# First feed-forward matrix in seven block products, its pairs taking turns with the second matrix's tiles, weight blocks added on VectorE

## The reference

```python
    x = x + mem_attend(rmsnorm(x, P['norm_mem']), mem_k, mem_v, P['mem_w_q'], P['mem_w_o'])
    h = rmsnorm(x, P['norm_ffn'])
    x = x + jnp.square(jax.nn.relu(h @ P['ffn_w1'])) @ P['ffn_w2']
```

## Time and profile before

| | |
|---|---|
| time, median of 3 runs | 1926.37 us (1924.69 to 1928.71) |
| span of the profiled execution | 1995.0 us, mean granted clock 0.878 |
| PE busy | 1911.0 us (96%) |
| DVE busy | 1020.3 us (51%) |
| ACT busy | 725.8 us (36%) |
| POOL busy | 105.2 us (5%) |
| first layer's feed-forward stage | about 608 to 1020 us |
| second layer's feed-forward stage | about 1591 to 1979 us |

### The profile page before, as it was taken

How to read it: one execution, slowest core, us unless ns; L and a number is a source line. 1 busy time by engine, 2 the same in 40 slices (tenths; PEclk the granted TensorE clock), 3 DMA queues, 4 the chain that set the end, 5 groups by cost and what they waited for, 6 DMA issues and landing times.

```text
span 1995.0 us, 37755 instructions
## 1 busy us (share of the span) xinstructions
PE 1911.0 (96%) x16626; PEld 1758.6 (88%) x16626; DVE 1020.3 (51%) x1741; ACT 725.8 (36%) x1268; POOL 105.2 (5%) x108
## 2 busy tenths in 40 slices
PE   6999998999999999999999999889999999999997
PEld 5985776999789999999999857769997999999996
DVE  6677665454335544344355776655543455353533
ACT  4434546452334221222234345453623432121222
POOL 2020000200010000000010200001000100000001
PEclk8888887888888888888888889989999999999998
DMA  5100000553112222222221000014520222222221
GB/s 218 59 17 1 4 24 24 194 171 104 33 64 75 85 85 85 85 75 87 83 78 60 19 1 3 3 46 155 194 85 22 85 85 88 93 85 85 96 85 56
DMA packets 38594, 149.52 MB, mean 75 GB/s; under 512 B 4384, under 2 KB 4544, under 8 KB 36768
## 3 DMA queue, kind: packets, MB, share of 16 engines
q1 hardware_dynamic: 36288, 131.05, 19.6%
q0 software_dynamic: 2144, 16.06, 2.2%
HBM read 139.68 MB, written 7.41 MB: 74 GB/s over the span
## 4 chain that ended last, share of the span: by engine, by line
PE 89%; DVE 4%; ACT 4%; issue 1%; POOL 1%; DMA 0%; DVEq 0%; SPq 0%; ACTq 0%; POOLq 0%
PE PS L651 82%; PE PS L789 5%; PE PS L1037 1%; ACT hH L1180 1%; POOL sq L577 1%; DVE stat L1968 1%; PE PS L1136 0%; DVE hL L1621 0%; DVE rs L1935 0%; DVE hT L1934 0%; ACT aP L1180 0%; ACT L1180 0%; POOL msq L629 0%; DVE wL L1607 0%; DMA mem<-mem_in 0%
## 5 line engine op out<-in xcount | busy, mean ns | idle before, releaser
L651 PE MATMUL PS<-hH,wH 128*128 128x272 f32 x2272 | 508.6, 307 | 32.2 <-DVE hL L1616 23.0
L651 PE MATMUL PS<-hH,wL 128*128 128x272 f32 x2272 | 488.7, 298 | 0.0
L651 PE MATMUL PS<-hL,wH 128*128 128x272 f32 x2272 | 488.3, 298 | 0.0
L651 PEld LDWEIGHTS PS<-hH,wH 128*128 128x128 f32 x2272 | 372.1, 194 | 51.9 <-issue 20.5
L1607 DVE TENSOR_TENSOR wL<-ring,wH 128x1024 fp32r<-128x1024 f32 x238 | 301.1, 1266 | 218.8 <-ACT wH L1180 218.4
L1180 ACT ACTIVATE wH<-ring 128x1024 fp32r<-128x1024 f32 x238 | 249.8, 1050 | 354.4 <-PE PS L651 352.7
L651 PEld LDWEIGHTS PS<-hH,wL 128*128 128x128 f32 x2272 | 370.3, 193 | 0.0
L651 PEld LDWEIGHTS PS<-hL,wH 128*128 128x128 f32 x2272 | 369.3, 193 | 0.0
L651 PE MATMUL PS<-hidH,wH 128*128 128x272 f32 x1024 | 216.6, 294 | 0.0
L651 PE MATMUL PS<-hidL,wH 128*128 128x272 f32 x1024 | 216.4, 293 | 0.0
L651 PE MATMUL PS<-hidH,wL 128*128 128x272 f32 x1024 | 216.2, 294 | 0.0
(11 more groups left out here) (322 smaller groups left out, 2630.6 us busy)
## 6 DMA issues: line engine op xcount, KB each, us to landing
ring<-wall SPq DMA_DIRECT2D x238, 512.0 KB, 3.3
lw<-lw_in POOLq DMA_DIRECT2D x2, 2240.0 KB, 9.6
xT<-x_in SPq DMA_DIRECT2D x4, 544.0 KB, 6.1
y_out<-hT SPq DMA_DIRECT2D x8, 272.0 KB, 2.1
mem<-mem_in POOLq DMA_DIRECT2D x2, 1024.0 KB, 5.1
mks<-mks_in POOLq DMA_DIRECT2D x2, 1024.0 KB, 10.5
mvs<-mvs_in POOLq DMA_DIRECT2D x2, 1024.0 KB, 13.4
memk_out<-mkp POOLq DMA_DIRECT2D x2, 1024.0 KB, 5.4
```

What stands on the lines that cost most here:

```text
L651: return e.matmul(out, lhsT=a, rhs=b, start=start, stop=stop)
```

## The change

The first feed-forward matrix is taken in pairs of output tiles, q = 0 to 15. A pair is a 2 x 2 block matrix (two halves of the 1024 inputs, two output tiles), and so are the activations (two halves of the inputs, two halves of the frames). Instead of eight block products the pair takes seven, on sums and differences of the blocks. A product is one unit: 4 blocks of 128 x 128, three products each, 272 frames, so 12 matmuls. The units are named M1, M5, M6, M2, M7, M4, M3 in the order in which they run; some go into the same PSUM bank on top of an earlier one, after ACT has copied out the sum so far.

- Weights: the pair's two loads (a, b) are split by halves of a tile. DVE computes four sums or differences of 128 x 512 numbers per pair (`combine`, called comb0 to comb3 below): one before each of M5, M6, M7, M3. Seven halves are split instead of two whole tiles. `wH` and `wL` now hold six halves.
- Ring: load a of a pair is given up after M2's half is split and after comb3; load b after M4's half. The next pair's load b takes the slot of this pair's load a.
- Activations: for each `mo` tile ACT writes two blocks (`up_raw`), DVE makes two differences (tiles 0 to 3) or three (tiles 4 to 7), ACT rounds and DVE subtracts the blocks (`up_hi`, `up_lo`). This takes the place of the eight `hH`, `hL` tiles behind `mo` 7.
- Results: ACT copies out of PSUM after M1, M6 and M7 (`f_a1`, `f_u2`, `f_u3`); DVE adds after M2, M7 and M3, and multiplies the positive part by `rs` in three instructions. ACT then squares twice (`squared`), once rounded and once not. DVE's `hid_lo` stays.
- Order: pairs 0 to 3 run alone, as M5 M6 M2 M7, M1 of the next pair, M4 M3. From pair 4 on two `f2` tiles stand in each pair: M1 M5 M6 M2 M7, f2, M4 M3, f2. The last eight `f2` tiles are as before.
- `lw` of the second layer is loaded after the first layer's last `f2` tile, in two parts, since its room now holds `hid`.

```diff
+def _ffn_units():
+    def up(q, *products):
+        return [("f1", 7 * q + j) for j in products]
+    units = up(0, M1)
+    for q in range(4):
+        units += up(q, M5, M6, M2, M7) + up(q + 1, M1) + up(q, M4, M3)
+    for q in range(4, PAIRS):
+        i = 2 * (q - 4)
+        units += (up(q, M1) if q > 4 else []) + up(q, M5, M6, M2, M7) + [("f2", i)] + up(q, M4, M3) + [("f2", i + 1)]
+    return units + [("f2", i) for i in range(8 * GROUPS - 8, 8 * GROUPS)]
...
+        def wait_raw_read(e, m):
+            l, (st, i) = m // NT, LOADS[m % NT]
+            if st != "f1":
+                e.wait_ge(w_lo, tile_no(l, st, i) + 1)
+            elif i % 2:
+                e.wait_ge(w_lo, tile_no(l, st, 7 * (i // 2) + M4) + 1)
+            else:
+                e.wait_ge(w_lo, tile_no(l, st, 7 * (i // 2) + M2) + 1)
+                e.wait_ge(s["comb"], at(l, "comb", 4 * (i // 2) + 4))
...
@@ tensor: up(l, i)
+                elif j == M6:
+                    e.wait_ge(s["f_a1"], at(l, "f_a1", q + 1))
+                elif j == M7:
+                    e.wait_ge(s["f_u2"], at(l, "f_u2", q + 1))
+                elif j == M4:
+                    e.wait_ge(s["f_u3"], at(l, "f_u3", q + 1))
+                else:
+                    e.wait_ge(s["f_c22"], at(l, "f_c22", q + 1))
...
@@ scalar
                 for i in range(8):
                     ahead(l, "mo", i)
-                    if i == 7:
-                        wait_tile(e, l, "mo", 7)
-                        for k in range(7):
-                            scaled_hi(l, "g_ffn", k)
                     wait_evac(e, l, "mo", i)
+                    up_raw(i)
                     square(3 * l + 2, i)
...
+                for st, i in FFN:
+                    ahead(l, st, i)
+                    if st == "f1":
+                        q, j = i // 7, i % 7
+                        if 0 < q < 5 and j in (M5, M6):
+                            squared(2 * (q - 1) + (j == M6))
+                        if (q, j) == (0, M7):
+                            rstd(3 * l + 2)
+                        if j in (M1, M6, M7):
+                            wait_tile(e, l, "f1", i)
+                            act(hid_part(q, j == M7, j != M1), up_bank(l, q, 0), ACT.Copy)\
+                                .then_inc(s[{M1: "f_a1", M6: "f_u2", M7: "f_u3"}[j]], 1)
...
@@ vector: combine(l, q, i)
+                if i == 0:
+                    wait_load(e, second)
+                    tt(sums[:, 0, :], raw_half(second, 0), raw_half(second, 1), ALU.add)\
...
+                elif i == 1:
+                    tt(sums[:, 1, :], sums[:, 0, :], raw_half(first, 0), ALU.subtract)\
...
+                elif i == 2:
+                    tt(raw_half(second, 0), raw_half(first, 0), raw_half(second, 0), ALU.subtract)\
...
+                else:
+                    tt(sums[:, 1, :], raw_half(first, 1), sums[:, 1, :], ALU.subtract)\
```

More of the change, by code:

```diff
@@ L68 @@
 N_IN = len(IN)
[L69 to L77, removed]
[L78 to L82 removed]
+DENSE = [(st, i) for st, n in (("in", N_IN), ("out", 8), ("mk", 8), ("mv", 8), ("mq", 8), ("mo", 8)) for i in range(n)]
@@ new lines, with _loads, _placed @@
+FFN = _ffn_units()
+UNIT_LIST = DENSE + FFN
+NU = len(UNIT_LIST)
+UNIT = {u: i for i, u in enumerate(UNIT_LIST)}
+def _loads():
+    loads = []
+    for st, i in UNIT_LIST:
+        if st != "f1":
+            loads.append((st, i))
+        elif i % 7 == M1:
+            loads += [("f1", 2 * (i // 7)), ("f1", 2 * (i // 7) + 1)]
+    return loads
+LOADS = _loads()
+NT = len(LOADS)
+LOAD = {t: i for i, t in enumerate(LOADS)}
+RING = 3
+HALVES = 6
+def _placed():
+    half, freed, parity, owner, at_, normal = [], [], [], [-1] * HALVES, 0, 0
+    for n in range(DEPTH * NU):
+        wide = UNIT_LIST[n % NU][0] != "f1"
+        at_ += wide and at_ % 2
+        mine = [at_ % HALVES] + [at_ % HALVES + 1] * wide
+        half.append(mine[0])
+        freed.append(max(owner[h] for h in mine))
+        for h in mine:
+            owner[h] = n
+        at_ += len(mine)
+        parity.append(normal % 2 if wide else None)
+        normal += wide
+    return half, freed, parity
@@ new lines @@
+HALF, FREED, PARITY = _placed()
+BEFORE = [max((m for m in range(n) if PARITY[m] == PARITY[n]), default=None) for n in range(DEPTH * NU)]
+FIRST_UNITS = [0, 1] + [l * NU + UNIT[("out", i)] for l in range(DEPTH) for i in range(2)]
+SPLITS_AT = {}
+for _u in range(DEPTH * NU):
+    if _u not in FIRST_UNITS:
+        SPLITS_AT.setdefault(FREED[_u] + 1, []).append(_u)
+EVAC_ENGINE = {st: "act" if st in ("mk", "mv") else "dve" for st, _ in UNIT_LIST}
+EVACUATED = [t for t in UNIT_LIST if t[0] != "f1" and (t[0] != "mv" or t[1] % 2)]
@@ L83, with evac_value @@
 EVAC_PER_LAYER = {e: sum(EVAC_ENGINE[t[0]] == e for t in EVACUATED) for e in ("act", "dve")}
-RUNS = [(0, N_IN), (N_IN, NT + N_IN), (NT + N_IN, 2 * NT)]
-def evac_value(layer, tile):
-    eng = EVAC_ENGINE[STREAM[tile][0]]
+def evac_value(layer, unit):
+    eng = EVAC_ENGINE[UNIT_LIST[unit][0]]
     return eng, layer * EVAC_PER_LAYER[eng] + sum(
-        EVAC_ENGINE[t[0]] == eng and t in EVACUATED for t in STREAM[:tile + 1])
+        EVAC_ENGINE[t[0]] == eng and t in EVACUATED for t in UNIT_LIST[:unit + 1])
@@ L569, in put, with add_squares @@
                 e.dma_start(out, src).then_inc(stored[kind], 16)
-            def add_squares(r):
-                for k in range(1, 8):
+            def add_squares(r, first=1, last=7):
+                for k in range(first, last + 1):
                     e.wait_ge(s["sq_ready"], 8 * r + k + 1)
@@ L727, in mem_product, with dense_steps @@
                     last.then_inc(pe_done, 1)
[L729 to L734, removed]
+            def dense_steps(l, st, one=None, h_from=0, first=0):
+                for i in range(first, {"in": N_IN}.get(st, 8)) if one is None else (one,):
+                    n = tile_no(l, st, i)
                     e.wait_ge(w_lo, n + 1)
-                    if n >= 2:
-                        eng, v = evac_value((n - 2) // NT, (n - 2) % NT)
+                    if BEFORE[n] is not None:
+                        eng, v = evac_value(BEFORE[n] // NU, BEFORE[n] % NU)
                         e.wait_ge(evac[eng], v)
@@ L1567, in _ @@
                     wait_evac(e, l, "mo", i)
+                    up_raw(i)
                     square(3 * l + 2, i)
[L1569 to L1587, removed]
+                    if i < 4:
+                        e.wait_ge(s["f_cross"], at(l, "f_cross", i + 1))
+                        up_hi(i, Q11, T2)
+                    else:
+                        e.wait_ge(s["f_turn"], at(l, "f_turn", 2 * i - 7))
+                        up_hi(i, T2, Q21)
+                        e.wait_ge(s["f_turn"], at(l, "f_turn", 2 * i - 6))
+                        up_hi(i, Q21, T4 + 1)
```

323 lines of the change are left out of this document (243 added, 80 removed).

## The result

| | before | after |
|---|---|---|
| time, median | 1927.54 us (1924.69 to 1930.62) | 1940.53 us (1937.07 to 1943.48) |
| ratio after / before | | 1.0067, 95% interval 1.0047 to 1.0088 |
| profiled execution: span, mean granted clock | 1995.0 us, 0.878 | 1935.3 us, 0.978 |

The change makes the kernel 13 us slower. I had forecast 1926 us, practically no change. The time lies in my range (1898 to 1944), but the slowdown, clear of the noise, is not what I had forecast. The profiled spans can't be compared, since the clocks differ.

A forecast was written before the change was run, and what follows sets the result against it. PE was taken as the bound. Fewer matmuls saved 25.5 us (first layer) and 24.0 (second), added stalls cost 17.4 and 23.7; twice the second layer's -0.3 gave 1926.4 - 0.6, 1926 us, range 1898 to 1944.

The forecast's parts named there:

- stage against before: First mo residual to last f2 residual of a layer; forecast net -8.1 us first layer, -0.3 second.
- the price of the mo tiles: DVE and ACT steps per mo tile: 5.2 us for tiles 0 to 3, 7.0 for 4 to 7, nothing for POOL's additions.
- The half clock: Rival, chance 0.12: after stalls PE's matmuls come 0.227 us apart, costing 5 to 8 us a layer; 1938 us.
- The slot of load b: In pairs 0 to 3 comb0 waits 3.3 us for load b; slower rival, chance 0.18: 4.2 or 5.3, 1934 to 1942 us.
- the list on DVE: DVE's instructions and waits in pairs 0 to 3 set the pace: 14.1 us a pair against PE's 10.5.
- the two long stalls: PE in the first pair waits for ACT's copies: 7.2 us ahead of M6, 6.4 us ahead of M4.
- the table loads: Two on ACT within rs, ahead of M7's copy, 1.28 us each, part of 3.95 us.
- the dense f2 phase: From pair 4 on, with two f2 tiles in each pair of 22.5 us: no PE loss.
- the late `lw`: Second layer's lw loads behind the first layer's last f2 tile; first used 12 us later, so costed at nothing.
- The drain of 1.38 us: The skill's drain at ACT table switches would lengthen M4's stall 2.8 us a layer, 1932 in all; forecast left it out.

The follow-up runs named there:

- e1: Changed kernel, but POOL's additions of squares in the mo tiles cover only 8 of 544 columns: 1930.43 us, ratio to before 1.0017.
- e5: The kernel before, unchanged, profiled once more: 1928.9 us, span 1926.8, clock 0.987.
- e2: Changed kernel, but in mo tiles 4 to 7 ACT squares behind its last rounding, so POOL adds later: 1942.85 us, ratio to before 1.0068.
- e9: Changed kernel, plus 44 matmuls of 128 columns on PE behind M1 of pair 1, ahead of M4: 1939.15 us, ratio to before 1.0055.
- e3: Changed kernel, but comb3 moved right behind comb2, so that load a's slot is free sooner: 1906.49 us, ratio to before 0.9877.
- three small moves: Changed kernel with comb3 right behind comb2, squares summed on PE, and rs made ahead of M6's copy: 1894.26 us, ratio to before 0.9824.

## Why the prediction was wrong

Times in the second layer, counted from M1's start (1523.14 in the changed kernel, t = 0 of the forecast):

| step | forecast | measured |
|---|---|---|
| 192 matmuls fewer, no loss from pair 4 on | 24.0 us saved | no gap; 0.1260 us a matmul for 0.1255 |
| mo tiles 0 to 3 | 5.2 us each | 5.2 |
| mo tiles 4 to 7 | 7.0 us each | 8.0 |
| M6 resumes | 9.9 | 13.6 |
| M4 resumes | 23.2 | 27.3 |
| DVE enters pair 1's list | 28.8 | 34.2 |
| pairs 1 and 2 | 14.1 us each | 14.7, 14.6; first layer 14.2, 14.1 |
| first f2 tile | 76.2 | 82.9; first layer 81.6 |
| stage against before | -0.3 us | +6.7 us; first layer +5.4 |

**The step that failed** is the price of the mo tiles. Of the 6.7 us by which the first f2 tile is late (5.4 in the first layer), 3.7 are there in both layers when M6 resumes. I had the row that tells it: DVE's instruction stretched from 1.23 to 1.55 us beside POOL. In its place I wrote "in the new order mostly one that waits for ACT anyway stands beside them, so I add nothing", and kept 1 us a layer for the range. It was 1.15 us in each of four tiles, 4.3 to 4.9 us a layer by e1. The 0.32 us of the row was no price per addition. It was what was left of the addition when DVE's instruction came. The pair of rows in the kernel before, profiled again (e5):

```profile
1488.79 1.36 POOL L577 TENSOR_TENSOR sq<-sq 128x544 f32<-128x544 f32 x1 [110.78 <-ACT sq L1180]
...
1489.69 1.54 DVE L1607 TENSOR_TENSOR wL<-ring,wH 128x1024 fp32r<-128x1024 f32 x1 [1.68 <-ACT wH L1180]
```

Here 0.46 us of the addition are left when DVE's instruction starts, and it loses 0.31. In the changed kernel 1.29 are left, and the third difference loses 1.16. In e2 it is 1.31 and 1.16. The new order has an instruction come 0.12 us behind the addition's start, so nearly all of it is left. With the stall ahead of M6 as it is, these microseconds go straight to the first f2 tile.

**The half clock** I had as a rival with a price of 5 to 8 us a layer. Behind M6's stall it lasts for 24 matmuls in both layers and costs nothing, since ACT's copy for M4 comes later still. Behind M4's stall it cost up to 1.7 us in the second layer and 0.1 in the first (e9). Behind the short stalls of pairs 1 to 3 it came once a layer, not in every pair. In the second layer that was in pair 1, for 16 matmuls, and the list on DVE hid all but 0.2 us. In the first it was in pair 3, for 14, and there DVE waits for PE at M3's sum, which it doesn't in the second layer's pair 3:

```profile
651.81 0.44 DVE L2363 TENSOR_TENSOR hT<-PS,hT 128x272 f32<-128x272 f32 x1 [0.68 <-PE PS L940]
...
1599.43 0.44 DVE L2363 TENSOR_TENSOR hT<-PS,hT 128x272 f32<-128x272 f32 x1
```

From DVE's entry into pair 3's list to the first f2 tile it is 20.4 us in the first layer and 19.4 in the second. I take the lower clock as the cause of this 1.0 us; no run takes it away by itself.

**The slot of load b** held in mechanism: comb0 stands for 1.9 to 2.3 us in each of the eight places. From comb3's end to comb0 it is 3.4 us in the first layer and 3.7 in the second, where I had 3.3; that makes the pairs 14.1 to 14.7 us long, and the rival's 4.2 and 5.3 didn't come. But e3 shows what I hadn't seen: the wait was there to be taken away by moving one instruction.

**Right** were the list on DVE and its 14 us a pair, what stands ahead of the two long stalls, the table loads, the dense f2 phase and the late `lw`. The loads take 1.28 us each, and the exponential starts 0.02 us behind the second. The drain of 1.38 us that the Trainium skill has there ("ScalarE: Activation LUTs", What ACT_TABLE_LOAD costs) isn't in this trace, as the forecast had said.

**The sum.** In the second layer the first f2 tile is 6.7 us late: 3.7 at M6, 0.4 more at M4 (the load's 3.6 us for 3.3), 1.3 more when DVE enters pair 1's list (the lower clock), and 1.3 in pairs 1 to 3, nearly all of it the load. In the first layer the same steps are 3.7, 0.3, 0.1 and 1.4, of which I put 1.0 down to the lower clock in pair 3. That makes 5.4, but for rounding.

**Not explained** is a small one: PE takes 6.055 us for an f2 tile in the changed kernel and 6.01 before, at the same granted clock of 1.00. The kernel before has 6.05 too in its mo tiles; only its f1 and f2 tiles take 6.01. Over the 2436 matmuls from the first to the last f2 residual that is 1.1 us a layer. With the 6.7 it is 7.8, against 7.0 missed in the second layer, and 6.5 against 5.7 in the first; the 0.8 between is open in both. I didn't try to find the cause.

## What to carry to other kernels

Where GpSimd works beside a dense list on VectorE whose operands lie in SBUF, price its instruction at its full length on that list, and look at who starts first in the new order, not at the stretch which the old order showed. A step that waits for a ring slot should free it as soon as its last reader can run: moving one subtraction up, to right behind comb2, was worth more than twice what the whole change had lost. And when a change turns a PE-bound stage into a chain over two engines, count the chain once more after each fix: here three small moves turned 13 us lost into 35 gained.

## What the runs showed of the hardware

- DVE and GpSimd took turns, whole instruction by whole instruction, wherever both had two operands in SBUF. A DVE difference of 272 columns took 0.44 us alone and 1.60 behind a GpSimd addition of 1.41. In e2, where DVE came first, GpSimd took 1.92, and then the next DVE instruction, already issued, waited for that (1.85 for 0.69).
- A matmul of 128 columns took 0.11 us at the upper clock (5.03 us for 44, granted clock 1.00), almost as long as one of 272 (0.126). Each has its own load of weights, 20 of them in 2.33 us. Which of the two sets the 0.11 isn't shown.
- After stalls of much the same length ahead of the same matmuls (3.89 and 4.24 us between two starts) the lower clock lasted for 12 matmuls in the first layer and 24 in the second. A stall's price can't be read from one place.
